# Two transformer blocks on one core: sums of squares, scaled tiles in PSUM and layer normalisations in another order

## The reference

```python
def rms_norm(x, g):
    return x * lax.rsqrt(jnp.mean(x * x, axis=-1, keepdims=True) + EPS) * g

# first block, three times
x = x + rms_norm(hybrid_mixer(rms_norm(x, ...)), norm_mix_post)
x = x + rms_norm(memory_cross_attention(rms_norm(x, ...), ...), norm_mem_post)
x = x + rms_norm(squared_relu_mlp(rms_norm(x, ...)), norm_mlp_post)

# second block, for i in (0, 1): an attention (MLA), then a Hyena mixer
x = layer_norm_2(DEEPNORM_ALPHA * x + m, ln1_g[i], ln1_b[i])
x = layer_norm_2(DEEPNORM_ALPHA * x + conv_ffn(x, ...), ln2_g[i], ln2_b[i])

def layer_norm_2(x, g, b):
    mu = mean(x); var = mean(square(x - mu))
    return (x - mu) * lax.rsqrt(var + NORM_EPS) * g + b
```

## Time and profile before

| | us |
|---|---|
| median of 3 runs | 2280.18 |
| profiled execution | 2287.43 |
| its span | 2285.6 |
| TensorE matmuls busy | 2118.8 (93%) |
| VectorE busy | 1327.9 (58%) |
| GpSimd busy | 942.6 (41%) |
| ScalarE busy | 842.3 (37%) |

### The profile page before, as it was taken

One profiled execution on the slowest core, in us unless ns is written; L12 is line 12 of the kernel. 1 busy time (PEld: TensorE's weight loads), 2 busy tenths in 40 slices (PEclk: granted clock), 3 DMA queues, 4 the chain that ended last, 5 costly groups with the idle time before them and its releaser, 6 DMA issues.

```text
span 2285.6 us, 23112 instructions
## 1 busy us (share of the span) xinstructions
PE 2118.8 (93%) x9481; PEld 1725.2 (75%) x9481; DVE 1327.9 (58%) x1596; ACT 842.3 (37%) x1195; POOL 942.6 (41%) x388
## 2 busy tenths in 40 slices
PE   8999978788999998899989999999988789999997
PEld 5677757666888886677778887887877677887786
DVE  7775760526234543356267777436678827777644
ACT  4623454463122224467243333224322324333322
POOL 4352144535444445211434444444666434444442
PEclk9998869898999998899989999999999989999998
DMA  5321102211322221111212222224231222222321
GB/s 199 136 107 57 56 19 74 74 56 56 107 95 92 92 99 66 40 40 46 74 53 95 92 92 101 103 74 157 92 119 57 111 74 74 92 92 95 108 92 37
DMA packets 34558, 194.02 MB, mean 85 GB/s; under 512 B 3903, under 2 KB 4495, under 8 KB 14932
## 3 DMA queue, kind: packets, MB, share of 16 engines
q1 hardware_dynamic: 34452, 192.54, 24.1%
HBM read 178.82 MB, written 13.64 MB: 84 GB/s over the span
## 4 chain that ended last, share of the span: by engine, by line
PE 59%; DVE 23%; ACT 11%; POOL 4%; issue 2%; DMA 0%; SPq 0%; DVEq 0%; POOLq 0%; ACTq 0%
PE ps L128 54%; DVE TMP L157 9%; DVE TMP L163 6%; PE ps L127 5%; ACT WH L144 4%; DVE TMP L151 1%; ACT TMP L145 1%; POOL X L151 1%; POOL WL L151 1%; ACT PAD L144 1%; PE ps L136 1%; DVE X L151 1%; DVE VG L151 1%; POOL YF L151 1%; POOL TMP L151 1%
## 5 line engine op out<-in xcount | busy, mean ns | idle before, releaser
L151 POOL TENSOR_TENSOR WL<-W,WH 128x2048 fp32r<-128x2048 f32 (+3 forms) x175 | 707.0, 4045 | 1044.9 <-ACT WH L144 1044.9
L128 PE MATMUL ps<-HH,WL 128*128 128x512 f32 x1456 | 585.6, 402 | 55.9 <-issue 14.4
L128 PE MATMUL ps<-HL,WH 128*128 128x512 f32 x1456 | 576.4, 396 | 0.0
L128 PE MATMUL ps<-HH,WH 128*128 128x512 f32 x1456 | 575.5, 395 | 0.0
L144 ACT ACTIVATE WH<-W 128x2048 fp32r<-128x2048 f32 (+2 forms) x157 | 291.8, 1859 | 321.8 <-PE ps L128 321.8
L128 PEld LDWEIGHTS ps<-HH,WL 128*128 128x128 f32 x1456 | 279.7, 192 | 128.4 <-issue 50.4
L128 PEld LDWEIGHTS ps<-HH,WH 128*128 128x128 f32 x1456 | 279.3, 192 | 60.2
L128 PEld LDWEIGHTS ps<-HL,WH 128*128 128x128 f32 x1456 | 280.3, 192 | 56.5 <-issue 0.2
L151 DVE TENSOR_TENSOR MRL<-MID,MRH 128x512 fp32r<-128x512 f32 x76 | 177.4, 2366 | 162.6 <-ACT MRH L144 162.6
L157 DVE TENSOR_SCALAR TMP<-PAD,PAR 128x512 f32<-128x512 f32 x88 | 209.0, 2375 | 70.6 <-ACT PAD L144 70.6
L128 PE MATMUL ps<-MRH,WL 128*128 128x512 f32 x608 | 238.3, 392 | 4.5 <-DVE TMP L163 2.3
(11 more groups left out here) (338 smaller groups left out, 3181.5 us busy)
## 6 DMA issues: line engine op xcount, KB each, us to landing
W<-in_up SPq DMA_DIRECT2D x44, 1024.0 KB, 4.9
W<-in_down SPq DMA_DIRECT2D x22, 1024.0 KB, 4.8
W<-in_w_up SPq DMA_DIRECT2D x16, 1024.0 KB, 4.8
W<-in_w_down SPq DMA_DIRECT2D x16, 1024.0 KB, 4.8
W<-in_hy_in SPq DMA_DIRECT2D x12, 1024.0 KB, 4.9
kd<-STG SPq DMA_DIRECT2D x36, 256.0 KB, 2.0
KB<-kd SPq DMA_DIRECT2D x8, 1024.0 KB, 5.1
W<-in_win_ag SPq DMA_DIRECT2D x4, 1024.0 KB, 4.8
```

The lines of the kernel that those rows point to most:

```text
L128: return self.eng.matmul(out, lhs, rhs, start=start, stop=stop)
L151: return QUIET if self.eng is None else self.eng.tensor_tensor(out, a, b, op)
```

## The change

- **Squares.** GpSimd adds squares 0 to 5 (five additions, not six); TensorE's column sums take DG, tile 6 and tile 7. In the layer norms the order becomes DG, square of tile 6, X of tile 7, square of tile 7.
- **Scaled tiles in PSUM.** In post, VectorE writes scaled tiles 0 and 1 into a reserved PSUM bank (yp), one after the other, and adds from there. The bank is taken in turn ahead of the column sums.
- **Layer norms.** VectorE takes the mean off two tiles ahead of the scaling, the first two before rstd is there. For tile 0 ScalarE writes only HH, straight from the scaled X; VectorE applies gain and bias to X itself (a tensor_scalar) and makes the low part of tile 0. VectorE makes low parts 0, 1, 3, 5, GpSimd 2, 4, 6, 7.
- **d = 3.** ScalarE copies the spreads of mean and rstd to SBUF (RS, DG); GpSimd takes the mean off tiles 6 and 7 and scales them, VectorE does tiles 0 to 5 and waits for the copies.

```diff
             def post(s, name):
-                column_sum([(("ys", s), DG, ("yacc", s, 6), None, None),
+                reserve("yp", s)
+                close("yp", s)
+                column_sum([(("ys", s), DG, ("yacc", s, 5), None, None),
+                            (("ys", s), tmp(name, 6), ("ysq", s, 6), (name, 6), None),
                             (("ys", s), tmp(name, 7), ("ysq", s, 7), (name, 7), ("ys", s))])
...
-                column_sum([(ds, X[:, 7, :], ("cx", d, 7), None, ds), (dq, DG, ("qacc", d, 6), None, None),
+                column_sum([(dq, DG, ("qacc", d, 5), None, None),
+                            (dq, tmp("dc", d, 6), ("dcq", d, 6), ("dc", d, 6), None),
+                            (ds, X[:, 7, :], ("cx", d, 7), None, ds),
                             (dq, tmp("dc", d, 7), ("dcq", d, 7), ("dc", d, 7), dq)])
...
+                if not split:
+                    act.wait_ge(*at("mu", d))
+                    act.copy(RS[:], bank("mu", d)[:]).then_inc(*out(("mus",)))
+                    act.wait_ge(*at("rstd", d))
+                    act.copy(DG[:], bank("rstd", d)[:]).then_inc(*out(("rstds",)))
                 for k in range(8):
                     act.wait_ge(*at("xn", d, k))
+                    if split and k == 0:
+                        act.act(HH[:, 0, :], X[:, 0, :], ACT.Identity, par(g), par(b)).then_inc(
+                            *out(("hn", 4 + d, 0, "hi")))
+                        continue
...
+                dve.wait_ge(*at("free", *earlier["yp", s]))
                 for k in range(10):
                     if k < 8:
+                        yn = Y[:, k, :] if k > 1 else bank("yp", s)[:]
...
+                        if k == 1:
+                            dve.wait_ge(*at("xr", s, 0))
+                        dve.stt(yn, Y[:, k, :], par(g, k), bank("rps", s)[:], ALU.mult, ALU.mult).then_inc(
...
+                n = 8 if split else 6
+                def centred(k):
+                    dve.wait_ge(*at("mu", d))
+                    dve.tt(X[:, k, :], X[:, k, :], bank("mu", d)[:], ALU.subtract).then_inc(
+                        *out(("xm", d, k), *[("free", "mu", d)] * (k == n - 1)))
+                if not split:
+                    dve.wait_ge(*at("mus"))
+                centred(0)
+                centred(1)
                 for k in range(9):
+                    if k < n:
+                        dve.wait_ge(*at("xm", d, k))
+                        dve.wait_ge(*at(*(("rstd", d) if split else ("rstds",))))
                         dve.tt(X[:, k, :], X[:, k, :], bank("rstd", d)[:], ALU.mult).then_inc(
+                            *out(("xn", d, k), *[("free", "rstd", d)] * (k == n - 1)))
+                    if split and k == 1:
+                        dve.wait_ge(*at("hn", 4 + d, 0, "hi"))
+                        dve.ts(X[:, 0, :], X[:, 0, :], par(g), par(b), ALU.mult, ALU.add).then_inc(*out(("x1", d, 0)))
+                        dve.wait_ge(*at("x1", d, 0))
+                        low(HL[:, 0, :], X[:, 0, :], HH[:, 0, :], ("hn", 4 + d, 0))
+                    if k + 2 < n:
+                        centred(k + 2)
                     j = k - 1
-                    if split and j in (1, 3, 5, 6, 7):
+                    if split and j in (1, 3, 5):
                         low(HL[:, j, :], X[:, j, :], HH[:, j, :], ("hn", 4 + d, j))
...
             def deep_norm(d):
-                for j in (0, 2, 4):
+                for j in (2, 4, 6, 7):
...
             deep(3, 0, 7)
+            for k in (6, 7):
...
+                pool.tt(X[:, k, :], X[:, k, :], RS[:], ALU.subtract).then_inc(*out(("xm", 3, k)))
+                pool.wait_ge(*at("xm", 3, k))
+                pool.wait_ge(*at("rstds"))
+                pool.tt(X[:, k, :], X[:, k, :], DG[:], ALU.mult).then_inc(*out(("xn", 3, k)))
```

More of the change, by code:

```diff
@@ L1955, in post @@
                 inverse(("ys", s), 8, [("col", "rps", s)])
+                dve.wait_ge(*at("free", *earlier["yp", s]))
                 for k in range(10):
                     if k < 8:
+                        yn = Y[:, k, :] if k > 1 else bank("yp", s)[:]
                         dve.wait_ge(*at("rps", s))
                         dve.wait_ge(*at("y", s, k))
-                        dve.stt(Y[:, k, :], Y[:, k, :], par(g, k), bank("rps", s)[:], ALU.mult, ALU.mult).then_inc(
+                        if k == 1:
+                            dve.wait_ge(*at("xr", s, 0))
+                        dve.stt(yn, Y[:, k, :], par(g, k), bank("rps", s)[:], ALU.mult, ALU.mult).then_inc(
                             *out(("yn", s, k), *[("free", "rps", s)] * (k == 7)))
@@ L1963, in post @@
                         dve.wait_ge(*at("yn", s, k))
-                        dve.tt(X[:, k, :], X[:, k, :], Y[:, k, :], ALU.add).then_inc(*out(("xr", s, k)))
+                        dve.tt(X[:, k, :], X[:, k, :], yn, ALU.add).then_inc(
+                            *out(("xr", s, k), *[("free", "yp", s)] * k))
                     else:
@@ L2182, in deep_norm @@
                 dve.recip(SM[:, 20:24], va).then_inc(*out(("col", "rstd", d)))
-                for k in range(9):
[L2184 to L2189, removed]
-                        dve.tt(X[:, k, :], X[:, k, :], bank("rstd", d)[:], ALU.mult).then_inc(
-                            *out(("xn", d, k), *[("free", "rstd", d)] * (k == 7)))
+                g, b = (("ln1_g0", "ln1_b0"), ("ln2_g0", "ln2_b0"), ("ln1_g1", "ln1_b1"), ("ln2_g1", "ln2_b1"))[d]
+                n = 8 if split else 6
[7 more added lines that the diff above has]
+                centred(1)
+                for k in range(9):
+                    if k < n:
+                        dve.wait_ge(*at("xm", d, k))
+                        dve.wait_ge(*at(*(("rstd", d) if split else ("rstds",))))
+                        dve.tt(X[:, k, :], X[:, k, :], bank("rstd", d)[:], ALU.mult).then_inc(
+                            *out(("xn", d, k), *[("free", "rstd", d)] * (k == n - 1)))
[6 more added lines that the diff above has]
+                        centred(k + 2)
                     j = k - 1
-                    if split and j in (1, 3, 5, 6, 7):
+                    if split and j in (1, 3, 5):
                         low(HL[:, j, :], X[:, j, :], HH[:, j, :], ("hn", 4 + d, j))
@@ L2417, in squares @@
             def squares(s, name, start, end):
-                add_up(DG[:], lambda n: tmp(name, n)[:], min(end, 6), ("ysq", s), ("yacc", s), (name,), start)
+                add_up(DG[:], lambda n: tmp(name, n)[:], min(end, 5), ("ysq", s), ("yacc", s), (name,), start)
             def post(s, Y):
@@ L2435, in pool_program @@
             weights(CH["w_down"][-1] + 1)
-            squares(3, "y3", 1, 6)
+            squares(3, "y3", 1, 5)
             weights(CH["w_down"][-1] + 2)
@@ L2441, in deep @@
             def deep(d, start, end):
-                add_up(DG[:], lambda k: tmp("dc", d, k)[:], min(end, 6), ("dcq", d), ("qacc", d), ("dc", d),
+                add_up(DG[:], lambda k: tmp("dc", d, k)[:], min(end, 5), ("dcq", d), ("qacc", d), ("dc", d),
                        max(start, 1))
             def deep_norm(d):
-                for j in (0, 2, 4):
+                for j in (2, 4, 6, 7):
                     pool.wait_ge(*at("hn", 4 + d, j, "hi"))
@@ L2515, in pool_program @@
             deep(3, 0, 7)
+            for k in (6, 7):
+                pool.wait_ge(*at("mus"))
+                pool.wait_ge(*at("cx", 3, k))
+                pool.wait_ge(*at("dcq", 3, k))
+                pool.wait_ge(*at("ds", 3))
+                pool.tt(X[:, k, :], X[:, k, :], RS[:], ALU.subtract).then_inc(*out(("xm", 3, k)))
+                pool.wait_ge(*at("xm", 3, k))
+                pool.wait_ge(*at("rstds"))
+                pool.tt(X[:, k, :], X[:, k, :], DG[:], ALU.mult).then_inc(*out(("xn", 3, k)))
         def sync_program(sp):
```

## The result

The changed kernel has a median of 2293.62 us (2291.51 to 2303.55, 6 runs) beside 2280.14 us for the kernel before on the same chip (6 runs): ratio 1.0062, interval 1.0046 to 1.0078. It is slower by 13.5 us by the medians and 14.1 by the ratio, where the prediction had 10.85.

What follows compares the result with a forecast made beforehand. The chain of waits was 59% TensorE, mostly matrix work left untouched. Terms -0.5 - 2.0 - 0.35 + 3.9 + 7.1 + 3.3 - 0.6 = +10.85 us on 2280.18 gave 2291.0, range 2277 to 2297.

Steps and rivals of the forecast that it cites:

- The stands: First three layer norms (1147, 1534, 1874 us): TensorE idles for GpSimd's late weight chunk, 3.8 us each.
- The clock: Behind each such TensorE idle in the first three layer norms the granted clock falls: 1.7 us (bounds 0 and 1.9).
- the clock did not hold: Rival: clock holds through the idles of the first three layer norms, 1.7 us less each, total 2285.9; chance 0.17.
- the stands are there: Rival on the faster side: weight chunk not late in the first three layer norms, total 2275.9; chance 0.15.
- the loops did not take them up: Rival: loops behind first and third layer norms absorb the whole idle, only the second pays, 2283.8; chance 0.13.
- The 0.6 taken off in d2: Third layer norm (1874 us): 0.6 us less cost because the clock had already dropped there before, leaving +3.3.
- The sums of the layer norms: Column sums of the four layer norms, eight more TensorE instructions each: about 0, +1.6, about 0, +1.1 us.
- Of which 16 can run earlier: Layer norms: 16 of 32 sum instructions can run before tile 7, so about 0 in first and third.
- b1 and b3: RMS boundaries at 408 and 880 us: -0.5 (bounds -0.9 and +0.4) and -0.35 us (-0.9 and +0.5).
- The meeting of GpSimd and VectorE: RMS boundaries: each GpSimd addition meeting VectorE's SBUF additions costs 0.42 us; two avoided give -0.84.
- b2: RMS boundary at 510 us: sums end 0.65 sooner, first low half about 2.1; -2.0 us (bounds -0.7 and -3.9).
- The end: Last layer norm (2262 us): tiles shared over VectorE, GpSimd and ScalarE, -1.7 us; with sums of +1.1, -0.6.

Runs made afterwards that it cites:

- b1_control: The changed kernel again with no edit, for a second profile: 2291.88 us, ratio 1.0048 to the kernel before.
- b3_rms_only: The kernel before with only the RMS part of the change (squares split, scaled tiles 0 and 1 in PSUM): 2278.65 us, ratio 0.9982.
- b4_end_only: The kernel before with only the last layer norm's tiles changed, its column sums as before: 2278.86 us, ratio 0.9986.
- c3_no_mean_ahead: The kernel before with the RMS part and the end of the change, without mean ahead or new tile 0: 2275.88 us, ratio 0.9976.
- a3_deep_squares_back: The changed kernel with the layer norms' split of squares undone, GpSimd adding tiles 0 to 6 again: 2287.0 us, ratio 1.0022.
- a4_no_psum: The changed kernel without the PSUM bank for scaled tiles 0 and 1, written to SBUF again: 2297.25 us, ratio 1.0067.
- c4_own_bank: The changed kernel with one PSUM bank skipped before the column sums of the first and third layer norms: 2288.78 us, ratio 1.0037.
- c1_gate: b2_both_back plus a GpSimd wait for VectorE's last square addition at the RMS boundary at 510 us: 2273.94 us, ratio 0.9969.
- a1_lows_back: The changed kernel with low halves of tiles 6 and 7 moved back from GpSimd to VectorE: 2281.1 us, ratio 0.9995.
- b2_both_back: The changed kernel with the undoings of a1_lows_back and a3_deep_squares_back together: 2272.77 us, ratio 0.9963.

## Why the prediction was right, and where it was not

The forecast was 2291.0, with a range to 2297 and a chance of 0.67 for slower; the medians are 2293.6 and 2291.9.

The parts of the layer norms can be told apart with all traces, not b1_control alone. "Rest" compares four traces with the old tiles (before, b3_rms_only, b4_end_only, c3_no_mean_ahead) and five with the tiles of the changed kernel (the first profile, a3_deep_squares_back, a4_no_psum, b1_control, c4_own_bank). "Way" compares eight traces with the old sums and five or six with the new ones. In us, range and mean:

| part | old code | changed code | difference | forecast |
|---|---|---|---|---|
| rest, d0 to d1 | 382.8 to 383.6 (383.0) | 386.7 to 387.9 (387.5) | +4.5 | +3.9 |
| rest, d1 to d2 | 333.0 to 333.9 (333.4) | 337.4 to 339.6 (338.4) | +5.0 | +5.5 |
| rest, d2 to d3 | 382.8 to 383.6 (383.0) | 386.6 to 387.5 (387.0) | +4.0 | +3.3 |
| way, d0 | 4.9 to 6.2 (5.5) | 6.7 to 7.0 (6.9) | +1.4 | 0 |
| way, d1 | 4.8 to 6.9 (5.7) | 5.7 to 8.5 (7.1) | +1.4 | +1.6 |
| way, d2 | 5.9 to 6.1 (6.0) | 7.7 to 7.8 (7.8) | +1.7 | 0 |
| way, d3 | 4.8 to 6.6 (5.6) | 5.7 to 6.5 (6.2) | +0.6 | +1.1 |

**The stands (d0, d1, d2).** This step held as worked out: 13.4 us against 12.7. GpSimd's chunk starts 16.7 us after the first scaling (16.8 forecast) and ends at 22.3 (22.8). TensorE ends chunk 0 at 18.3 (18.0) and stands 4.1 to 4.3 us. The forecast's own clock gives a stand of 4.8 (18.0 to 22.8); its 3.8 is the delay of chunk 1 against 19.0, and that came out at 3.4. The clock: behind the stands in b1_control 10, 9 and 6 matmuls start 0.43 us behind the one before, the first of each 0.56; over 0.23 each that is 2.5, 2.3 and 1.6 us, where 1.7 was forecast. Undoing this part alone gave back 12 to 15 us, doing it alone cost 9 by the ratio and 13.4 by the rest. The rivals fall: the clock did not hold in any of the three, the stands are there, and the loops did not take them up: d0 and d2 cost 4.5 and 4.0 beside d1's 5.0. The loops take up 1 us at most, less than the 1.6 that the forecast itself took off for them in each of d0 and d2. The mistake in that rival: the loop's period is set by its own work, and behind a late start it runs at the same pace, so it repays nothing. The 0.6 taken off in d2 for a clock that "had already dropped there before" came from one execution: only the profile before has that fall (0.67, last section).

**The sums of the layer norms.** "Of which 16 can run earlier", and so "about 0" in d0 and d2, was the step that failed. I had looked at what data the products need, not at what their bank needs: the group of squares takes the bank of the mean estimate, which the centring of tile 7 frees. The table of banks can be followed from open_bank. It costs 1.4 us in d0 and 1.7 in d2. In d1 and d3, where I had 1.6 and 1.1, it is 1.4 and 0.6; there the way varies by 2 us and more with the level of the clock, and one pair of traces can't size it. Together about 5 us against 2.7, which is within the doubt of the 6 and 9 us by the medians of a3_deep_squares_back.

**b1 and b3.** The meeting of GpSimd and VectorE was sized right: -0.89 against -0.84, and +0.35 for the sums of b1 is what the rows show (square of tile 7 to root 1.49 us, before 1.14). What I had left out is the clock behind them: 1.3 us more in b1, in seven of ten traces, and 1.6 in b3, in all of them. In b3 the sum itself was off by a little: +0.45 - 0.84 is -0.39, not -0.35. The 1.6 us don't need the PSUM bank: a4_no_psum has them too (43.99 us from b3 to n3, 45.6 before). In b3 the old code stood 2.81 us for a weight chunk and then ran at half clock; TensorE's timelines and windows, first b4_end_only, then b1_control:

```profile
920.75 0.47 PE L128 MATMUL ps<-HH,WL 128*128 128x512 f32 x1 [2.81 <-POOL WL L151]
...
921.00:924.00 3.00, 3.00 (x9) 2.28 (x9) 0.00 (x0) 0.00 (x0) 3.00 (x2) 0.53 0.51 175
```

```profile
918.85 0.47 PE L128 MATMUL ps<-HH,WL 128*128 128x512 f32 x1 [2.08 <-POOL WL L151]
...
919.00:922.00 3.00, 3.00 (x14) 2.48 (x15) 0.00 (x0) 0.00 (x0) 3.00 (x2) 1.00 0.62 180
```

**b2.** The sums end 0.5 us sooner behind the last square (0.65 forecast), but n1 to b2 shrinks by 0.1 only, as the granted clock over that stretch is 0.92 and not 0.94. Low half 0 does come 2.1 us sooner in b1_control, yet 0.9 of it is that VectorE's first scaling starts 0.9 sooner behind the root (1.72 and not 2.64 us); in c1_gate it starts at 2.65, and TensorE gains 0.9 and not 2.1. But -2.0 was reckoned against a trace in which the last square addition was already blocked by GpSimd's next piece. Two other executions of the same code slipped it in ahead (28.26 us, not 30.30). The changed kernel moved the meeting so that it is blocked in all its traces. Against the state of before that two of three traces show the stretch costs 1.1 us; one profile can't show that a row is one of two outcomes of a race.

**The end.** -1.4 us in the changed kernel and -1.8 alone, against -1.7. Ten operations take 6.07 us, 0.61 each. By the rule of the Trainium skill (VectorE: DVE Perf Modes, The DRAIN you can't avoid), measured there on copies, they would have cost up to 0.9 more, an estimate; here operations whose waits lie two behind are quicker than the 0.66 of before, so the measurement decides against it for this case.

**The sum.** The RMS boundaries gave some 3.9 us (4.2 in the stretches, less 0.35 for the sum ahead of b1's root) and not 2.85, the sums of the layer norms cost some 5 and not 2.7, the stands and tiles 13.4 and not 12.7, the end gave 1.4 and not 1.7. That makes 13.2, beside 11.0 and 14.1 us by the two ratios. The stands, most of the total, were forecast with their cause. That the total is nearer than its smaller terms is luck: the RMS gain and the cost of the sums were both forecast too small, with opposite signs.

## To carry to other kernels

Before work is moved onto an engine, lay its queue out between the time its inputs are there and the time its output is wanted: what doesn't fit there is late in any order, and a hole behind it costs clock on TensorE as well. Before a group of products is counted as hidden, ask which bank it takes and who frees it. And read a stretch of a microsecond in several traces before a term is built on it: whether two engines meet on a port, and how soon the clock comes back, can change from one execution to the next.

## What the runs showed of the hardware

**Which stands cost clock.** Stands of 2.08 us (b1_control, b3) and 2.48 us (a4_no_psum, b3) left the clock at its full level of 2.4 GHz; one of 2.14 us (a1_lows_back, d1) was followed by a mean of 0.71 over 5 us, and one of 2.81 us by the level of 1.2 GHz. All stands of 4.1 us and more were followed by the lower one. Between 2.1 and 2.5 us the length of the stand alone doesn't decide. The plainest pair is one place of one code, d2 with the old layer norm, in two executions: TensorE's timeline and the window behind it, first before, then b3_rms_only:

```profile
1898.17 0.50 PE L128 MATMUL ps<-HH,WL 128*128 128x512 f32 x1 [2.12 <-DVE HL L151]
...
1898.00:1903.00 5.00, 4.83 (x13) 3.53 (x14) 2.59 (x4) 0.77 (x2) 2.94 (x2) 0.67 0.17 29
```

```profile
1891.59 0.50 PE L128 MATMUL ps<-HH,WL 128*128 128x512 f32 x1 [2.11 <-DVE HL L151]
...
1891.00:1896.00 5.00, 4.39 (x18) 3.31 (x19) 3.27 (x4) 1.82 (x4) 3.37 (x2) 1.00 0.13 20
```

The rest of d2 to d3 is 383.57 us in the first and 382.81 in the second. The windows of TensorE in d1, first a1_lows_back behind 2.14 us, then b2_both_back behind 1.81 us at the same place of d1:

```profile
1551.00:1556.00 5.00, 3.84 (x11) 2.96 (x12) 2.80 (x2) 1.16 (x3) 3.94 (x3) 0.71 0.74 315
```

```profile
1547.00:1552.00 5.00, 4.10 (x16) 3.04 (x17) 3.26 (x4) 1.82 (x4) 3.66 (x3) 1.00 0.75 315
```

One such fall costs 0.8 us in the pair of d2 and some 2 in d1 of a1_lows_back (rest 334.2 us, 331.8 and 331.9 in b2_both_back and c1_gate), as much as most edits here. It is one reason why stretches with the same code differ by up to 2 us in some traces and by less than 0.1 in others.
